# Standing weights in alternate words and moving activations read backwards, in a two-block transformer kernel on one core

## The reference

```python
# first block
mod = silu(c) @ w_ada + b_ada                    # shift, scale, gate
h = rms(x, norm_g) * (1 + scale) + shift
a_q, a_k, a_v, a_z, g_q, g_f, g_i, g_z = split(h @ w_in)        # 2048 -> 8192
att = chunk_attention(a_q, a_k, a_v) * silu(a_z)                # 8 heads
hg  = hgrn2(g_q, g_f, g_i) * silu(g_z)                          # gated recurrence, 8 heads
x = x + gate * (concat(att, hg) @ w_out)
# second block
z = rms(x, g_mix) @ w_in_2                       # pooling, two latents, rope key, cross query
y = concat(pool_mixer, latent_attention, memory_cross_attention) @ w_o_2
x = x + y
h = rms(x, g_ffn)
x = x + (silu(causal_conv3(h @ w_gate) + conv_b) * (h @ w_up)) @ w_down    # 2048 -> 5632 -> 2048
```

## Time and profile before

| | |
|---|---|
| Runs | 1596.76 us median of 3 (1593.56 to 1600.59) |
| Profiled execution, own time | 1599.0 us |
| Its span, first to last instruction | 1599.0 us |
| Instructions | 24289, 9650 of them matmuls and as many weight loads |
| Busy | PE 1573.0, PEld 1400.7, DVE 1154.1, ACT 862.4, POOL 151.6 us |
| Mean granted clock of TensorE | 0.994 of 2.4 GHz |
| Loaded from memory | 327.37 MB, 206 GB/s over the span |

### The profile page before, as it was taken

One profiled execution on the slowest core, in us unless ns is written; L12 is line 12 of the kernel. 1 busy time (PEld: TensorE's weight loads), 2 busy tenths in 40 slices (PEclk: granted clock), 3 DMA queues, 4 the chain that ended last, 5 costly groups with the idle time before them and its releaser, 6 DMA issues.

```text
span 1599.0 us, 24289 instructions
## 1 busy us (share of the span) xinstructions
PE 1573.0 (98%) x9650; PEld 1400.7 (88%) x9650; DVE 1154.1 (72%) x1696; ACT 862.4 (54%) x1321; POOL 151.6 (9%) x164
## 2 busy tenths in 40 slices
PE   8998999989999999999999999999999999999999
PEld 6787889988999999988799888888888888888887
DVE  6797867877778886759778777777777777455544
ACT  6855546767665555655556454544444444444442
POOL 0000000321221220034213000000000000000000
PEclk9999999999999999999999999999999999999999
DMA  9999975533457774343244545555455454555552
GB/s 373 369 343 349 365 285 209 188 114 121 180 189 267 285 272 179 132 158 132 97 144 178 189 170 199 184 186 210 172 197 191 179 211 175 205 199 185 198 196 105
DMA packets 47825, 331.02 MB, mean 207 GB/s; under 512 B 5281, under 2 KB 6689, under 8 KB 8417
## 3 DMA queue, kind: packets, MB, share of 16 engines
q1 hardware_dynamic: 45184, 312.20, 53.5%
q0 software_dynamic: 2240, 17.04, 2.8%
q10 hardware_dynamic: 290, 0.25, 0.1%
HBM read 327.37 MB, written 2.10 MB: 206 GB/s over the span
## 4 chain that ended last, share of the span: by engine, by line
PE 89%; DVE 5%; DMA 3%; ACT 2%; issue 1%; POOL 0%; SPq 0%; ACTq 0%; DVEq 0%; POOLq 0%
PE ps L1173 20%; PE ps L1174 11%; PE ps L1169 9%; PE ps L1170 8%; PE ps L1171 8%; PE ps L1228 5%; PE ps L1227 5%; PE ps L1226 5%; PE ps L1216 4%; PE ps L1217 3%; PE ps L1218 3%; DVE wl L1916 2%; DMA raw<-in_wts 1%; DMA xs<-in_xN 1%; PE ps L1384 1%; PE ps L1351 1%
## 5 line engine op out<-in xcount | busy, mean ns | idle before, releaser
L1916 DVE TENSOR_TENSOR wl<-raw,wh 128x1024 fp32r<-128x1024 f32 x512 | 626.2, 1236 | 282.4 <-ACT wh L1519 281.9
L1519 ACT ACTIVATE wh<-raw 128x1024 fp32r<-128x1024 f32 x512 | 531.3, 1054 | 377.2 <-PE ps L1228 130.6
L1173 PE MATMUL ps<-hA,wh 128*128 128x512 f32 x1408 | 488.7, 390 | 0.0
L1174 PE MATMUL ps<-hA,wl 128*128 128x256 f32 x1408 | 397.0, 282 | 0.0
L1173 PEld LDWEIGHTS ps<-hA,wh 128*128 128x128 f32 x1408 | 264.2, 188 | 55.3
L1174 PEld LDWEIGHTS ps<-hA,wl 128*128 128x128 f32 x1408 | 266.1, 189 | 0.0
L1169 PE MATMUL ps<-hA,wh 128*128 128x256 f32 x752 | 219.5, 292 | 0.0
L1170 PE MATMUL ps<-hA,wh 128*128 128x256 f32 x752 | 211.7, 282 | 0.0
L1171 PE MATMUL ps<-hA,wl 128*128 128x256 f32 x752 | 211.7, 282 | 0.0
L1169 PE MATMUL ps<-hB,wh 128*128 128x256 f32 x576 | 164.4, 285 | 0.8 <-DVE work L2362 0.4
L1170 PE MATMUL ps<-hB,wh 128*128 128x256 f32 x576 | 161.1, 280 | 0.0
(11 more groups left out here) (303 smaller groups left out, 2077.9 us busy)
## 6 DMA issues: line engine op xcount, KB each, us to landing
raw<-in_wts SPq DMA_DIRECT2D x256, 1024.0 KB, 4.8
raw<-in_ada SPq DMA_DIRECT2D x36, 1024.0 KB, 6.1
side<-in_ada POOLq DMA_DIRECT2D x12, 1024.0 KB, 8.5
work<-in_memN SPq DMA_DIRECT2D x2, 1024.0 KB, 8.9
xs<-in_xN POOLq DMA_DIRECT2D x1, 2048.0 KB, 20.6
xs<-in_xT POOLq DMA_DIRECT2D x2, 1024.0 KB, 7.8
out_rows<-xs SPq DMA_DIRECT2D x8, 256.0 KB, 2.4
wp<-in_dt SPq DMA_DIRECT2D x8, 128.0 KB, 2.7
```

The source lines that it names most:

```text
L1173: e.matmul(ps[bank][:, :], w1, hl, start=first, stop=False)
L1174: i = e.matmul(ps[bank][:, T:2 * T], w2, hl[:, 0:T], start=False, stop=last)
L1519: e.activation(wh[:, h % WS, :], raw[:, n % RAW, part * HALF:(part + 1) * HALF], ACT.Copy).then_inc(s_hi)
L1916: e.tensor_tensor(wl[:, h % WS, :], src, wh[:, h % WS, :].bitcast(F32), ALU.subtract).then_inc(s_lo)
```

## The change

It does four things. The high and low parts of a half lie in one buffer `wb`: for halves in which the weights stand, in alternate words (high in even words, low in odd); for halves in which the weights move (`moved`), in two contiguous rows, as before. In `s` halves the moving activations and the PSUM columns that they are written to are read and written from the last to the first. The second views begin 128 bytes on, in place of 32. And the mask table is packed to 128 + 7 x 64 bytes.

```diff
+VIEW = 128
...
+        self.moved = set()
...
     def m_half(...)        # likewise in chunk_half, memory_row, down_half
+        self.moved.add(h)
     def down_end(self, kts):
+        self.moved.update(range(h, h + 2 * len(kts)))
...
-        wh = sb("wh", [P, WS, HALF], F32R)
-        wl = sb("wl", [P, WS, HALF], F32R)
+        wb = sb("wb", [P, WS, 2 * HALF], F32R)
...
         hA = sb("hA", [P, KT, 512], F32R)
-        at[0] += 32
+        at[0] += VIEW
...
-        early = nc.alloc_sbuf_tensor_at("early", [P, 4096], F32, offset=at[0] + 32)
-        E1 = nc.alloc_sbuf_tensor_at("E1", [P, 512], F32, offset=at[0] + 32 + 15 * 2048)[:, :]
+        early = nc.alloc_sbuf_tensor_at("early", [P, 4096], F32, offset=at[0] + VIEW)
+        E1 = nc.alloc_sbuf_tensor_at("E1", [P, 512], F32, offset=at[0] + VIEW + 15 * 2048)[:, :]
         hB_off = at[0]
         hB = sb("hB", [P, KT, 512], F32R)
-        at[0] += 32
+        at[0] += VIEW
...
-        mk = sb("mk", [P, len(LEVELS), P], U8, 1)
+        mk = sb("mk", [P, P + 64 * (len(LEVELS) - 1)], U8, 1)
...
-        hA2 = nc.alloc_sbuf_tensor_at("hA2", [P, KT, 512], F32R, offset=hA_off + 32)
-        hB2 = nc.alloc_sbuf_tensor_at("hB2", [P, KT, 512], F32R, offset=hB_off + 32)
+        hA2 = nc.alloc_sbuf_tensor_at("hA2", [P, KT, 512], F32R, offset=hA_off + VIEW)
+        hB2 = nc.alloc_sbuf_tensor_at("hB2", [P, KT, 512], F32R, offset=hB_off + VIEW)
...
+        def weights(h):
+            slot = wb[:, h % WS, :]
+            if h in o.moved:
+                return slot[:, 0:HALF], slot[:, HALF:2 * HALF]
+            return slot[:, 0::2], slot[:, 1::2]
...
             def s(h, j, bank, buf, kt, first, last, tile, fresh):
-                w1, w2 = wh[:, h % WS, j * P:(j + 1) * P], wl[:, h % WS, j * P:(j + 1) * P]
+                w1, w2 = (w[:, j * P:(j + 1) * P] for w in weights(h))
...
-                    e.matmul(po, w1, hl[:, 0:T], start=first, stop=False)
-                    e.matmul(po, w1, hl[:, T:2 * T], start=False, stop=False)
-                    i = e.matmul(po, w2, hl[:, 0:T], start=False, stop=last)
+                    po, hi, lo = (x[:, ::-1] for x in (po, hl[:, 0:T], hl[:, T:2 * T]))
+                    e.matmul(po, w1, hi, start=first, stop=False)
+                    e.matmul(po, w1, lo, start=False, stop=False)
+                    i = e.matmul(po, w2, hi, start=False, stop=last)
                 else:
-                    e.matmul(ps[bank][:, :], w1, hl, start=first, stop=False)
-                    i = e.matmul(ps[bank][:, T:2 * T], w2, hl[:, 0:T], start=False, stop=last)
+                    e.matmul(ps[bank][:, ::-1], w1, hl[:, ::-1], start=first, stop=False)
+                    i = e.matmul(ps[bank][:, T:2 * T][:, ::-1], w2, hl[:, 0:T][:, ::-1], start=False, stop=last)
...
             def split(h, n, part):                      # on ACT
-                e.activation(wh[:, h % WS, :], raw[:, n % RAW, part * HALF:(part + 1) * HALF], ACT.Copy).then_inc(s_hi)
+                e.activation(weights(h)[0], raw[:, n % RAW, part * HALF:(part + 1) * HALF], ACT.Copy).then_inc(s_hi)
...
             def split(h, n, part):                      # on DVE
-                e.tensor_tensor(wl[:, h % WS, :], src, wh[:, h % WS, :].bitcast(F32), ALU.subtract).then_inc(s_lo)
+                hi, lo = weights(h)
+                e.tensor_tensor(lo, src, hi.bitcast(F32), ALU.subtract).then_inc(s_lo)
```

More of the change, by code:

```diff
@@ L1141, in _ @@
                 elif b[0] == "consts":
-                    e.dma_start(mk[:].rearrange("p a b -> p (a b)"), msk).then_inc(s_mask, 16)
+                    e.dma_start(mk[:], msk).then_inc(s_mask, 16)
                     e.dma_start(cs[:, P:], cst[:, P:]).then_inc(s_const, 16)
@@ L1182, in m @@
                 for j, kt in enumerate(kts):
-                    w1, w2 = wh[:, h % WS, j * 512:(j + 1) * 512], wl[:, h % WS, j * 512:(j + 1) * 512]
+                    w1, w2 = (w[:, j * 512:(j + 1) * 512] for w in weights(h))
                     if fresh[j]:
@@ L1203, in chunk @@
                     c = 2 * pair + i
-                    w1, w2 = wh[:, h % WS, i * 512:(i + 1) * 512], wl[:, h % WS, i * 512:(i + 1) * 512]
+                    w1, w2 = (w[:, i * 512:(i + 1) * 512] for w in weights(h))
                     if kt == kts[0]:
@@ L1221, in down_part @@
             def down_part(h, kt, c, t, first, last):
-                w1, w2 = (w[:, h % WS, c % 2 * 512:c % 2 * 512 + 512] for w in (wh, wl))
+                w1, w2 = (w[:, c % 2 * 512:c % 2 * 512 + 512] for w in weights(h))
                 hi = hB[:, kt % KT, t * P:(t + 1) * P]
@@ L2042, in pick @@
                         src = bank[:, :].rearrange("p (a w) -> p a w", a=4)
-                        mask = mk[:, 0, :].unsqueeze(1).broadcast_to([P, 4, P])
+                        mask = mk[:, 0:P].unsqueeze(1).broadcast_to([P, 4, P])
                     else:
@@ L2048, in pick @@
                         src = bank[:, 0:T].rearrange("p (a n w) -> p a n w", a=4, w=h)
-                        mask = mk[:, li, 0:64].rearrange("p (n w) -> p n w", w=h).unsqueeze(1).broadcast_to([P, 4, n, h])
+                        mask = mk[:, P + 64 * (li - 1):P + 64 * li].rearrange("p (n w) -> p n w", w=h).unsqueeze(1).broadcast_to([P, 4, n, h])
                     e.copy_predicated(dst, mask, src).then_inc(mark(t, "dve", ("p", li)))
@@ L2561, in constants @@
             m[:, n, 0:64] = (s // (2 * h) == late // (2 * h)) & (s % (2 * h) < h)
-    return c, m.reshape(P, -1)
+    return c, np.concatenate([m[:, 0]] + [m[:, n, 0:64] for n in range(1, len(LEVELS))], 1)
 def kernel(**inputs):
```

## The result

The changed kernel takes 1607.79 us (median of 5 runs, 1606.45 to 1610.72) against 1598.68 us before (5 runs, 1593.56 to 1600.94). The ratio is 1.0063, with a 95% interval of 1.0046 to 1.0081: slower by 9.1 us, small but clear. The forecast was 1553, faster; the time lies inside the range of 1528 to 1640, on the side of rival (b).

A forecast was written before the change was run, and what follows sets the result against it. TensorE's matmul pace was taken as the bound: 51.7 us of pace gain less 8 given back is 43.7 off 1599.0, so 1555. The runs' median lies 2.2 lower, giving 1553 us, range 1528 to 1640.

The forecast's parts named there:

- rival (b): On every load of L1169 to L1174 the read streams cross more often: slower, 1623 to 1674 us; chance 0.18.
- The bound and the place: Whole kernel: TensorE's matmul pace bounds it; 10 to 13 ns lost per weight load, depending on where operands lie.
- the change part by part: Standing-weight matmuls: equal-speed streams going the same way stay apart after one clash; 111.0 ns per 256 columns, 329 per pair.
- The floor: Clash-free pace taken from L1263: 109.4 ns per 256-column matmul, 325.4 per feed-forward pair.
- the sum: Gain in matmul pace: feed-forward 23.9 us, first views 13.8, second views 14.0, together 51.7.
- The views' move: Second views from 32 to 128 bytes on: nothing to 3.3 ns each way, costed apart from the order.
- First views: 1536 matmuls of f, q, z and az on first views: 120.0 to 111 ns, 13.8 us gained.
- Moved halves, DVE, the mask: Moved halves keep 226.7 ns; DVE's word-spaced access and the smaller mask table change nothing.
- ACT: ACT's word-spaced copies of high parts: taken as nothing; even double, 1054 ns more, would hide in the feed-forward stretch.
- Giveback: Gain lost again: 2 us between about 531 and 572 us, 6 us at the recurrence's small steps, 8 in all.
- Rival (c): Word-spaced loads or backward bank rows run at half pace: 2180 or 2500 us; chance 0.10 for both.
- Rival (a): Every load loses a fixed 10 ns, placement only 3.3: at most 5 us gained, 1592 to 1600; chance 0.12.

The follow-up runs named there:

- e1: Kernel before with only the standing weights' high and low parts in alternate words: ratio 1.0119, +17.8 us.
- e7: Kernel before with ACT and DVE writing alternate words, PE reading contiguous ones, plus one buffer and packed mask: ratio 1.0012, 1.9 us over.
- b1: Kernel before with second views 192 bytes on, feed-forward view at 32, first view's standing blocks 64 on: 1593.41 us against 1600.64, ratio 0.9959.
- b2: b1 with gate and up also at 192 bytes, in three matmuls of 256 columns: 1601.84 us, ratio 1.0008 to the kernel before.
- The map: Kernel before with gate and up tiles reading operands in 43 ways, as pairs or 256-column matmuls: 346.7 to 358.7 ns per pair in the ways shown.
- m2: Kernel before with gate and up tiles read in 43 ways, split into three 256-column matmuls: 113.3 to 123.7 ns each.
- m3: Kernel before with more moving-tile starts, shifted standing blocks and shifted down-product weights: 113.3 ns at start 112, down product 226.7 to 235.
- e3: Kernel before with only the second views moved to 128 bytes on: ratio 1.0062, +7.7 us.
- e4: Changed kernel with moving tiles and bank columns forward again: ratio 1.0136, +22.0 us to the kernel before.
- e6: Changed kernel with second views 32 bytes on again: ratio 1.0147, +23.9 us to the kernel before.

## Why the prediction was wrong

**The bound and the place: right.** The pace of the matmuls is what moves this kernel, and where operands lie sets it. The earlier trace rows against the earlier trace rows said so, and the changed kernel and e1 to e7 differ from before by what their paces give, within 3.2 us, b1 and b2 within 4.4.

**The step that failed** is the first one of "the change part by part": that two streams of equal speed going the same way keep their distance, so that a clash parts them for good. The forecast made this depend on loads walking backwards by nature. The map has spaced words with the tile forward and with the tile backward at nine starts each; whichever way a load walks, one of the two is the equal-speed case. Neither comes under 117.8 ns, where 111 was forecast, and the pair's one 346.7 is no better than before, where 329 was forecast. (That the two streams have equal speed was itself assumed: a load's record lasts 188 ns or more, and no run shows how fast it reads.) What the runs showed in its place: word-spaced loads take longer themselves, medians of 193 to 199 ns for 187 to 192, and every way falls into a steady pattern, most often of 340, 346.7, 350, 351, 353 or 360 ns per block, 371 at the worst. That is a table, and the change moved from one of its better cells to a middling one.

**The floor was taken from the wrong row.** 109.4 ns came from L1263, which transposes. Its weight loads are quicker, in the profile of the kernel before:

```profile
L1263 PEld LDWEIGHTS ps<-cs,xs x32: 139/140/143, 886.6 to 935.8; 128*128 128x128 f32 x32
```

140 ns where the float32r loads take 188 to 192, and the float32 loads of L1351, which does not transpose, 192. So the row has no loss to show for the loads in question; and that its columns pass in 106.7 ns, with 2.7 as a fixed part, was assumed: no run shows that split. No way of m2 or m3 took a 256-column matmul under 113.3. So 111 was not reached by any way tried, 329 for a pair neither, and of the 51.7 us in the sum about 2448 x 3.9 + 1536 x 6.5 = 20 us exist at the very best, none in the pair as it stands. The sum also took 116.7 ns for all second views from one stretch; their mean is 117.2.

**The views' move**, costed at nothing to 3.3 ns each way, cost 1.9 ns on second views and 4.4 on the pair when done alone (e3): per load that is 1.9 and 2.2, so the bound held, but the sum charged it to the second views alone and left the pair out.

**First views: no change.** Forecast 120.0 to 111, measured 120.05. Spacing and backward reading each change it or not (118.3 for rows backward), and together they land on the old value.

**Moved halves, DVE, the mask: right**, 226.7 ns and 1238 ns; the mask was not tested by itself, e7 has it and is 1.9 us over before in all. **ACT: mis-sized**, taken as nothing by DVE's rows where it is 89 ns per copy; hidden as argued, as far as e7 goes (62 ns of it, 1.9 us).

**Giveback**: not reached, as nothing was gained. In b1 11.4 us by pace became 7.2 measured, which may be such a giveback; b2 has a gap of the same size (3.2 us less by pace, 1.2 more measured) and no run says what it is.

**Rival (b)** had the sign, the place and the deciding point (a pace above 117 or a pair above 346), not the mechanism, a doubled number of crossings. The point was set too low to decide anything: by their class means, 117.2 and 346.8, the kernel before passes it too. Its prices were too high by a factor: 26 us for a third more, where 9 came. Rival (c) is refuted in both halves: loads went from 188 to 196 ns and not to double, and backward banks cost next to nothing (at most 0.9 ns in any case of the map). Rival (a), a fixed price per load, is right about the wide pair, whose loss of about 27 ns no way reduced, and wrong about the 256-column matmuls.

What stays open: whether and where in SBUF the two reads meet, and what decides into which of two patterns a stretch falls. The standing operand was never read in the opposite direction, and the loads' own direction is not shown.

## What to carry to other kernels

When PE is full and each matmul has its load, read the distance of two starts, not busy times, and look for the same instruction at two paces: the spread is the room that placement has, here 113 to 124 ns for 256 columns. Measure it as a table: one kernel whose tiles each read their operands another way gives 43 values in one run, and the pace times the count then foretold e4 and e6 to 3 us in 1600. It missed b1 by 5 us or more and b2 by over 20: the quick pattern did not last in the one and did not come in the other. Don't reason about one part at a time: three parts that each cost 7 to 18 us cost 9 together, and try the whole kernel before you count on a quick pattern.

## What the hardware showed that I had not expected

- Matmuls in a steady stream lock into patterns with a repeating cost, in steps of 3.3 ns per 256 columns or of fractions of it (113.3, 116.7, 117.8, 120.0), mostly periodic in 256 bytes of distance (119.9 at 0 and 256, 120.0 at 512 and 1024), and with two patterns at one distance (346.7 or 353.3, 113.3 or 118.0). A break of a few other matmuls, or a short wait, can switch between them (113.5 ns before one, 118.0 after it, in b1).
- A bank written from the last column to the first costs next to nothing (346.7 ns both ways; over four cases between 2.2 ns less and 0.9 more).
- A word-spaced standing operand lengthens its load, medians of 193 to 199 ns where contiguous ones have 187 to 192, and ACT's word-spaced copy by 62 to 97 ns of 1054 in the mean over all halves; DVE's subtraction reads and writes spaced words at no cost.
- The kernel before sat at a start that none of the others tried beats, for its wide pair and for the down product, and not for its 256-column matmuls.
